# Another order of woven work in the expert stage: the context mixer's convolution beside the second routing pass

## The reference, cut to what matters

```
q = (xc @ w_q).reshape(128, 8, 2, 128);  s = einsum('thid,hikd->thik', q, sub_keys)
s1, i1 = top_k(s[:, :, 0], 16);  s2, i2 = top_k(s[:, :, 1], 16)      # then the best 16 of the 16 x 16 sums
hid = gelu(einsum('td,thkd->thk', xc, u_emb[eidx]))
out = einsum('thk,thkd->td', softmax(top_s) * hid, v_emb[eidx])      # 128 experts a token
conv = (b_gate * depthwise_conv(c_gate * h, conv_w)) @ conv_out_w     # three taps, per channel
```

## Time and profile before

| | us |
|---|---|
| median of 3 runs | 4298.63 |
| profiled execution | 4305.71 |
| its span | 4303.7 |
| PE busy | 3739.0 (87%) |
| VectorE (DVE) busy | 2835.1 (66%) |
| ScalarE (ACT) busy | 1159.6 (27%) |
| GpSimd (POOL) busy | 903.0 (21%) |
| gather queue q0, weight queue q1, shares of 16 DMA engines' time | 46.1%, 26.2% |

### The profile page before, as it was taken

One profiled execution on the slowest core, in us unless ns is written; L12 is line 12 of the kernel. 1 busy time (PEld: TensorE's weight loads), 2 busy tenths in 40 slices (PEclk: granted clock), 3 DMA queues, 4 the chain that ended last, 5 costly groups with the idle time before them and its releaser, 6 DMA issues.

```text
span 4303.7 us, 42567 instructions
## 1 busy us (share of the span) xinstructions
PE 3739.0 (87%) x15389; PEld 2386.2 (55%) x15389; DVE 2835.1 (66%) x6600; ACT 1159.6 (27%) x2577; POOL 903.0 (21%) x772
## 2 busy tenths in 40 slices
PE   7999988778999877789896888777779989999898
PEld 3457454334745423345543554232239879898797
DVE  3241137988877798887875568886656576565764
ACT  2140021124111111231011422111124444444443
POOL 0000013433332344333431024544320000000000
PEclk9999999999999999999998899999999999999999
DMA  6363458987998999889995179999975534555343
GB/s 250 147 255 134 164 207 354 405 344 303 411 421 360 398 400 412 335 345 399 420 421 218 40 317 379 422 383 421 422 301 175 181 128 166 176 177 177 130 167 132
DMA packets 246622, 1225.90 MB, mean 285 GB/s; under 512 B 19256, under 2 KB 46202, under 8 KB 124428
## 3 DMA queue, kind: packets, MB, share of 16 engines
q0 software_dynamic: 110592, 805.36, 46.1%
q1 hardware_dynamic: 135820, 417.84, 26.2%
HBM read 1222.07 MB, written 1.05 MB: 284 GB/s over the span
## 4 chain that ended last, share of the span: by engine, by line
PE 39%; DMA 17%; DVE 16%; ACT 3%; issue 2%; POOL 1%; DVEq 0%; ACTq 0%; SPq 0%; POOLq 0%
PE ps L431 10%; DMA BIG<-in_t_uv,idx 10%; PE ps L799 7%; PE ps L800 7%; PE ps L801 7%; PE ps L774 6%; DMA gbuf<-in_t_uv,idx 4%; DMA wbuf<-in_t_uv,idx 2%; DVE BIG L1924 2%; DVE gbuf L1924 2%; DVE wbuf L1924 1%; PE ps L419 1%; DVE plo L1965 1%; DVE BIG L1917 1%; PE ps L424 1%
## 5 line engine op out<-in xcount | busy, mean ns | idle before, releaser
L431 PE MATMUL ps<-wbuf,BIG 128*128 128x512 f32 x1856 | 822.7, 600 | 10.2 <-ACT BIG L1206 4.4
L2745 POOL DMA_INDIRECT gbuf<-in_t_uv,idx x286 | 337.2, 1179 | 1455.3 <-DVE BIG L1837 829.5
L431 PEld LDWEIGHTS ps<-wbuf,BIG 128*128 128x128 f32 x1856 | 354.1, 193 | 451.2 <-issue 437.9
L1965 DVE TENSOR_TENSOR plo<-wbuf,phi 128x1024 fp32r<-128x1024 f32 (+1 forms) x344 | 401.6, 1180 | 288.5 <-ACT phi L1311 287.8
L774 PE MATMUL ps<-gbuf,BIG 128*128 128x512 f32 x868 | 436.9, 642 | 163.5 <-ACT BIG L1276 163.4
L774 PE MATMUL ps<-BIG 128*128 128x512 f32 x904 | 428.9, 613 | 113.8 <-ACT BIG L1276 113.6
L1291 ACT ACTIVATE BIG<-BIG 128x2 f32<-128x2 f32 x384 | 78.1, 203 | 1442.2 <-DVE BIG L1931 1434.2
L799 PE MATMUL ps<-XH,phi 128*128 128x256 f32 x1472 | 423.5, 288 | 25.2 <-DVE XL L1975 21.4
L1924 DVE CUSTOM_DVE_ANT_0 BIG<-BIG 128x1024 f32<-128x1024 f32 x292 | 355.6, 1221 | 122.6 <-DMA BIG<-in_t_uv,idx 122.0
L431 PE MATMUL ps<-BIG,wbuf 128*128 128x256 f32 (+1 forms) x2048 | 423.7, 368 | 0.4 <-DMA wbuf<-in_t_conv 0.3
L2745 POOL DMA_INDIRECT BIG<-in_t_uv,idx x292 | 341.0, 1168 | 390.3 <-PE ps L774 321.5
(11 more groups left out here) (361 smaller groups left out, 5066.2 us busy)
## 6 DMA issues: line engine op xcount, KB each, us to landing
wbuf<-in_t_in SPq DMA_DIRECT2D x84, 1024.0 KB, 8.9
wbuf<-in_ffn_wg SPq DMA_DIRECT2D x20, 2048.0 KB, 7.8
wbuf<-in_ffn_wu SPq DMA_DIRECT2D x20, 2048.0 KB, 7.7
wbuf<-in_t_conv SPq DMA_DIRECT2D x48, 768.0 KB, 8.6
wbuf<-in_t_w_mod SPq DMA_DIRECT2D x32, 1024.0 KB, 7.2
wbuf<-in_ffn_wd SPq DMA_DIRECT2D x16, 2048.0 KB, 8.0
wbuf<-in_t_peer_wq SPq DMA_DIRECT2D x24, 1024.0 KB, 7.0
wbuf<-in_w_in SPq DMA_DIRECT2D x14, 1536.0 KB, 6.6
```

The costliest lines, as they stand in the source:

```text
L431: ins = p(mm)(bank, l, r, start=(k == 0), stop=(k == 7))
L1965: v(tt)(lo, W2.of(key, rows_, n)[:, k0:k1, c0:c1], hi.bitcast(F32), ALU.subtract).then_inc(dve_piece.up(q), 1)
L2745: g(nc.gpsimd.indirect_dma_start)(slot, None, I["t_uv"], bass.IndirectOffsetOnAxis(ap=idx[:, tb % 3, j:j + 1], axis=0)).then_inc(g_landed[ ...
```

## The change

The three mixer functions are cut into pooled, convolution and gates on each engine and in the list of weight loads. For x of both layers the parts are called in the old order. For the context of layer 0:

- the convolution runs beside the second routing pass of A, by a new generator `alongside` (0.66 beats of it for each beat of the routing), with its own ring `side_b` of four places, and its result goes to `CV` at 0 and no more at 24576; its weight tiles are loaded ahead of the query tiles;
- the scale of the routing pass goes from 0.72 to 0.5, the convolution has 0.55, the rest of the mixer goes from 0.6 to 0.72, so that its queries and attention start later;
- the V sums of (A,1) with j < 24 are all on TensorE; the first on VectorE is j = 25;
- the gather ring holds {6, 8, 9} up to 99, {6, 7, 8, 9} from 100, {6, 7, 9} from 152, {7, 9} from 220, {7, 8, 9} from 340.

```diff
+def alongside(main, other, rate):
+    n = 0.0
+    for m in main:
+        yield m
+        n += rate * m
+        while n > 0:
+            k = next(other, None)
+            if k is None:
+                break
+            yield k
+            n -= k
+    yield from other
...
-        beside.QT, ..., beside.PL, beside.CV = by_col(24576), ..., by_col(10240), by_col(24576)
+        beside.QT, ..., beside.PL, beside.CV = by_col(24576), ..., by_col(10240), by_col(0)
...
-        side, side4 = Ring(sides), Ring(sides[0:4])
+        side, side4, side_b = Ring(sides), Ring(sides[0:4]), Ring(sides[4:8])
...
-                        if i == 1:
+                        if i == (25 if T == "A" else 1):
...
-            return (T, tb) not in SHARED or j % 4 == 0 or (T == "A" and j >= 104)
+            return (T, tb) not in SHARED or j % 4 == 0 or (T == "A" and (j < 24 or j >= 104))
...
         def pe_context(p):                     # the same in act_context and dve_context
             yield from pe_rest(p, "A", first.XT)
-            yield from scaled(pe_route_scores(p, "A", "A", 1), 0.72, 1)
-            yield from scaled(pe_beside(p), 0.6, 1)
+            route = scaled(pe_route_scores(p, "A", "A", 1), 0.5, 1)
+            yield next(route)
+            yield from alongside(route, scaled(pe_beside_first(p), 0.55, 1), 0.66)
+            yield from scaled(pe_beside(p), 0.72, 1)
             yield 6
             yield from scaled(pe_route_scores(p, "B", "A", 2, 0, 2), 0.6, 1)
...
+        def dve_beside_first(v):
+            v.wait_ge(*pe_peer.at("A", "pq", 3, 3))
+            side_b.reset((pe_route, ("A", 1, 12)))
+            yield from dve_conv(v, "B", 0, beside, side_b)
...
-                if s == 64:
-                    gat.held, gat.freed[6] = {8, 9}, ((pe_peer, ("A", "pq", 3, 3)),)
-                if s == 90:
-                    gat.held = {7, 8, 9}
-                if s == 140:
-                    gat.held, gat.freed[8] = {7, 9}, ((pe_att, ("B", 3, NH - 1, "s", 1)),)
+                if s == 100:
+                    gat.held = {6, 7, 8, 9}
+                if s == 152:
+                    gat.held, gat.freed[8] = {6, 7, 9}, ((pe_att, ("B", 3, NH - 1, "s", 1)),)
+                if s == 220:
+                    gat.held, gat.freed[6] = {7, 9}, ((pe_mix, ("B", "br", 1, 2, 1)),)
...
             sync_peer(s, "A", 0)
+            sync_conv(s, "B", 0)
             sync_qkv(s, "B", 0, 0, range(2))
-            sync_mixer(s, "B", 0)
+            sync_pooled(s, "B", 0)
+            sync_gates(s, "B", 0)
```

More of the change, by code:

```diff
@@ L317, in build @@
         first.XT, first.AT, first.t0 = first.xts[0], first.MM, 0
-        beside.QT, beside.MM, beside.UU, beside.PL, beside.CV = by_col(24576), by_tok(8192, 2), by_tok(24576, 2), by_col(10240), by_col(24576)
+        beside.QT, beside.MM, beside.UU, beside.PL, beside.CV = by_col(24576), by_tok(8192, 2), by_tok(24576, 2), by_col(10240), by_col(0)
         beside.XT, beside.AT, beside.t0 = beside.xts[1], beside.MM, 2
@@ L570, in pe_attention, with pe_pooled @@
                     yield 2
-        def pe_mixer(p, T, l, L):
-            XT, UU, PL, CV = L.XT, L.UU, L.PL, L.CV
+        def pe_pooled(p, T, l, L):
+            XT, UU = L.XT, L.UU
             for n in range(2):
@@ L592, in pe_mixer, with pe_conv @@
             W.done(("pool", T), pe_mix, T, "pl", 3, 1)
+        def pe_conv(p, T, l, L):
+            XT = L.XT
             for cb in range(8):
@@ L601, in pe_mixer, with pe_gates @@
                 halves_done(key, pe_mix, T, "cv", cb, 2)
+        def pe_gates(p, T, l, L):
+            XT, PL, CV = L.XT, L.PL, L.CV
             for n in range(2):
@@ L1107, in act_attention, with act_pooled @@
                     yield 2
-        def act_mixer(a, T, l, L, ring2, ring1):
+        def act_pooled(a, T, l, L):
             UU, PL = L.UU, L.PL
@@ L1125, in act_mixer, with act_conv @@
                         act_mix.up(T, "pl", g, cb), 1)
+        def act_conv(a, T, l, L, ring2):
             for cb in range(8):
@@ L1668, in dve_mixer, with dve_conv @@
                 yield 1
+        def dve_conv(v, T, l, L, ring2):
+            CV = L.CV
             for cb in range(8):
@@ L1689, in dve_mixer, with dve_gates @@
                 v(tt)(CV[:, cb, 0:256], b[2][:, 0:256], cc, ALU.mult).then_inc(dve_mix.up(T, "cv", cb), 1)
+        def dve_gates(v, T, l, L, ring1):
+            MM = L.MM
             for n in range(2):
@@ L2439, in tensor @@
             edge(p, ("attended", "A"))
-            run(pe_mixer(p, "A", 0, first))
+            run(pe_pooled(p, "A", 0, first))
+            run(pe_conv(p, "A", 0, first))
+            run(pe_gates(p, "A", 0, first))
             edge(p, "mixed A")
@@ L2473, in pe_context, with pe_beside_first @@
             yield from pe_rest(p, "A", first.XT)
-            yield from scaled(pe_route_scores(p, "A", "A", 1), 0.72, 1)
-            yield from scaled(pe_beside(p), 0.6, 1)
+            route = scaled(pe_route_scores(p, "A", "A", 1), 0.5, 1)
+            yield next(route)
+            yield from alongside(route, scaled(pe_beside_first(p), 0.55, 1), 0.66)
+            yield from scaled(pe_beside(p), 0.72, 1)
             yield 6
             yield from scaled(pe_route_scores(p, "B", "A", 2, 0, 2), 0.6, 1)
+        def pe_beside_first(p):
+            yield from pe_conv(p, "B", 0, beside)
         def pe_beside(p):
@@ L2485, in pe_beside @@
             edge(p, ("attended", "B"))
-            yield from pe_mixer(p, "B", 0, L)
+            yield from pe_pooled(p, "B", 0, L)
+            yield from pe_gates(p, "B", 0, L)
             yield from pe_mixer_end(p, "B", 0, L)
@@ L2504, in pe_tokens @@
             edge(p, ("attended", "C"))
-            yield from pe_mixer(p, "C", 1, L)
+            yield from pe_pooled(p, "C", 1, L)
+            yield from pe_conv(p, "C", 1, L)
+            yield from pe_gates(p, "C", 1, L)
         def scalar(a):
@@ L2532, in scalar @@
             fence(a, ("attended", "A"))
-            run(act_mixer(a, "A", 0, first, big, tmp))
+            run(act_pooled(a, "A", 0, first))
+            run(act_conv(a, "A", 0, first, big))
+            run(act_gates(a, "A", 0, first, tmp))
             fence(a, "mixed A")
@@ L2565, in act_context, with act_beside_first @@
             yield from act_rest(a, "A")
-            yield from scaled(act_route_pass(a, "A", 1, route_before("A", 1, 0)), 0.72, 1)
-            yield from scaled(act_beside(a), 0.6, 1)
+            route = scaled(act_route_pass(a, "A", 1, route_before("A", 1, 0)), 0.5, 1)
+            yield next(route)
+            yield from alongside(route, scaled(act_beside_first(a), 0.55, 1), 0.66)
+            yield from scaled(act_beside(a), 0.72, 1)
             yield 6
             yield from scaled(act_route_pass(a, "B", 2, route_before("B", 2, 0), 0, 2), 0.6, 1)
+        def act_beside_first(a):
+            yield from act_conv(a, "B", 0, beside, side_b)
         def act_beside(a):
@@ L2577, in act_beside @@
             edge(a, ("attended", "B"))
-            yield from act_mixer(a, "B", 0, L, side4, side4)
+            yield from act_pooled(a, "B", 0, L)
+            yield from act_gates(a, "B", 0, L, side4)
             yield from act_mixer_end(a, "B", 0, L, side4)
@@ L2597, in act_tokens @@
             edge(a, ("attended", "C"))
-            yield from act_mixer(a, "C", 1, L, side4, side4)
+            yield from act_pooled(a, "C", 1, L)
+            yield from act_conv(a, "C", 1, L, side4)
+            yield from act_gates(a, "C", 1, L, side4)
         def vector(v):
@@ L2624, in vector @@
             tmp.reset()
-            run(dve_mixer(v, "A", 0, first, big, tmp))
+            run(dve_pooled(v, "A", 0, first))
+            run(dve_conv(v, "A", 0, first, big))
+            run(dve_gates(v, "A", 0, first, tmp))
             fence(v, "mixed A")
@@ L2674, in dve_context @@
             yield from dve_rest(v, "A", 0)
-            yield from scaled(dve_route_pass(v, "A", 0, 1), 0.72, 1)
-            yield from scaled(dve_beside(v), 0.6, 1)
+            route = scaled(dve_route_pass(v, "A", 0, 1), 0.5, 1)
+            yield next(route)
+            yield from alongside(route, scaled(dve_beside_first(v), 0.55, 1), 0.66)
+            yield from scaled(dve_beside(v), 0.72, 1)
             yield 6
             yield from scaled(dve_route_pass(v, "B", 0, 2, 0, 2), 0.6, 1)
+        def dve_beside_first(v):
+            v.wait_ge(*pe_peer.at("A", "pq", 3, 3))
+            side_b.reset((pe_route, ("A", 1, 12)))
+            yield from dve_conv(v, "B", 0, beside, side_b)
         def dve_beside(v):
@@ L2689, in dve_beside @@
             side4.reset(*edges.events(("attended", "B")))
-            yield from dve_mixer(v, "B", 0, L, side4, side4)
+            yield from dve_pooled(v, "B", 0, L)
+            yield from dve_gates(v, "B", 0, L, side4)
             yield from dve_mixer_end(v, "B", 0, L, side4)
@@ L2711, in dve_tokens @@
             side4.reset(*edges.events(("attended", "C")))
```

(24 more changed lines are left out.)

4 lines of the change are left out of this document (2 added, 2 removed).

## The result

The changed kernel takes 4334.03 us (median of 4, 4326.6 to 4338.18) against 4299.04 (median of 4): ratio 1.0076, interval 1.0064 to 1.0089, some 33 us slower. Forecast was 4289.6, range 4270 to 4312. The direction was wrong, and the time lies above the range, also above the figure of rival 3, 4311.6.

A forecast was written before the change was run, and what follows sets the result against it. Each stage of the first 256 expert steps has another limit among PE, VectorE and DMA. Stages 209 + 52 + 80 + 181 + 115 + 73 = 710 against 719, -9 us, giving 4289.6 us on the median, range 4270 to 4312.

The forecast's parts named there:

- rival 3: Gather ring: six slots starve VectorE; +33 us in all, discounted by two thirds to +22, 4311.6 us; chance 0.21.
- A: Second routing pass, with the convolution moved in: 209 us against 152, +57, PE load 201.6.
- Rival 2: Second routing pass swallows the gain: it takes 218 us, the sum is 719, time 4298.6 us; chance 0.17.
- B1: Context queries, 11.5 steps: 52 us against 47, +5, slot cost included.
- E: Last stage of the 256 expert steps, after the mixer's end: 73 us against 71.
- the price of the six slots: Gather ring, gathers 100 to 151: 1 to 2 us in each of A and B1, some in B2's 80.
- C: Pooled part, convolution and gates, 48.9 steps in place of 69.5: 181 us, -82, full on PE and DMA.
- D: Mixer's end, norm, rows and routing queries: 115 us against 114, PE load 110, DMA 109.
- B2: Context attention, 23.6 steps: 80 us, +8, with VectorE load 67 and PE 71.
- time per step times places is the trip: Gather ring, used by rival 3: a slot's round trip over the number of slots gives the time per step.
- The gain of 9 us: First 256 expert steps: stage times sum to 710 us against 719, -9 us, forecast chance 0.42.
- The rule of the Trainium skill: DMA engines take queue rows in turn, so weight tiles moved into A delay gathers; not used in the sum.

The follow-up runs named there:

- e3: The kernel before with the changed kernel's gather slots, order and V sums as before; ratio to before 1.0071.
- e6: The changed kernel with the context's queries and up projections at 18432, so slot 7 stays with the gathers; ratio to before 1.0006.
- e7: e6 with V sums on TensorE for j < 16 instead of j < 24; ratio to before 0.9992.
- e8: e6 with the V sums of j < 24 on VectorE but each fourth, as in the kernel before; ratio to before 1.0026, 4312.83 us.

## Why the prediction was wrong, step by step

- *A: right.* Forecast 209, measured 207.2, with PE 200.3 busy of 208 for a load of 201.6. Rival 2 (A swallows the gain, 218) did not happen. *B1*: 52, measured 52.4. *E*: 73, measured 71.2.
- *The failed step is the price of the six slots*: "I took 1 to 2 us in each of A and B1 and some in B2's 80", and nothing in C and D. They cost 30 (e3, and e6 against the changed kernel). By stages the changed kernel is longer than e6 by 2.2 in A, 3.1 in B1, 9.9 in B2, 8.7 in C and 4.4 in D. The mechanism is the one of rival 3, which had the chance 0.21.
- *What the price overlooked*: gathers up to 151 belong to steps up to 151, the V sums of j < 24 start some five steps behind their dot products, and the up projections start at 149: the fewest slots, rows held longest and PE's longest products met there. In A at step 90 a V sum starts 10 us after its dot product, at steps 148 to 152 it is 24 to 27 us. And from 152 to 219 the change has seven places where before has eight, which the sum didn't name.
- *Rival 3's sum was no better, and its nearness is luck*: before its discount it had 33 us, but as 6 in A, 7 in B1 and 20 in B2, where the slots cost 15 in all; it had nothing for C and D, where they cost 13. The rule "time per step times places is the trip" was wrong for where the cost falls, and the discount to two thirds has no run for it.
- *C, 181*: right as a load, e7 took 178.1; the changed kernel's 196.4 holds the slots (8.7, against e6's 187.7) and the late V sums (9.6 more, against e7's 178.1), for which the sum had 5.
- *B2, 80*: too low by 16; with slot 7 restored it is 86. VectorE was 70 busy, as forecast (67); 28 us of landing waits in B and early C remain even with seven slots. The forecast had B1 and B2 at 5 and 8 over 47 and 72; by the cuts of the table before took 42.0 and 77.9, so that the agreement in B1 is in part one of the cuts.
- *D, 115*: too low by 16, and by 9 in e7; PE's load was right, its idle time at the mixer's end (17.5 to 22.7 us) was not thought of. I had looked at loads only. What makes that idle time is argued above, not shown.
- The gain of 9 us hung on stages' loads meeting without friction. The stages came to 754 against the forecast's 710. With slots and V sums put right (e7) steps 0 to 256 took 873.5 us against 874.9: the gain in C (84 us for 20.6 fewer steps) is paid in A (51), B (17) and D (15).
- The rule of the Trainium skill ("DMA: Bandwidth & Descriptors", Queues, rings and completion order) that the prediction weighed against the change spoke on the right side, but moving the tiles is not needed for the loss: e3 has the full cost with the weight tiles where they were. What the sharing of the DMA engines adds to a landing no run here tells apart.

## What to carry to other kernels

A ring of landing places has a round trip: landing time plus all that stands before the last reader. I would now count it from its parts, with the longest instruction group that the last reader's engine may run first (no run here tests that sum), in every stage in which places are fewer, and try the loss of a place by itself first, as e3 did. Before moving work to a stage with room, ask what room its results take from others until they are read: here a place of 8 KB a partition, held to gather 219, cost 30 us where the move was to bring 9. And look for chains that the slower order hid: an engine that is made less busy may arrive at them earlier and stand there.

## What was not expected of the hardware

- PE's granted clock in attention followed how much PE had to do there: 0.70 with a quarter of the V sums (e8, PE busy 62 of 97 us), 0.84 with nearly all and six places (changed, 75 of 97), 0.90 with nearly all and seven (e6, 73 of 86), for the same attention.
- Taking one place of 1 MB out of a ring of seven, later eight, cost 30 us; adding an eighth and ninth gained 5.
